# Convolution layers: where ScalarE empties the chain banks, where VectorE takes moments, and where two z products stand

## The reference, cut to what matters

```python
def conformer_conv_mixer(h, w_in, conv_w, conv_b, ln_g, ln_b, w_out):
    proj = h @ w_in
    val, glu_gate, z = jnp.split(proj, 3, axis=-1)
    u = val * jax.nn.sigmoid(glu_gate)
    u = causal_depthwise_conv(u, conv_w) + conv_b      # 31 taps per channel
    u = jax.nn.silu(layer_norm(u, ln_g, ln_b))
    return (u * jax.nn.silu(z)) @ w_out
```

## Time and profile before

| | us |
|---|---|
| median of 3 runs (2718.98 to 2719.5) | 2719.24 |
| the profiled execution | 2718.03 |
| its span, first to last instruction | 2716.3 |

### The profile page before, as it was taken

One profiled execution on the slowest core, in us unless ns is written; L12 is line 12 of the kernel. 1 busy time (PEld: TensorE's weight loads), 2 busy tenths in 40 slices (PEclk: granted clock), 3 DMA queues, 4 the chain that ended last, 5 costly groups with the idle time before them and its releaser, 6 DMA issues.

```text
span 2716.3 us, 31913 instructions
## 1 busy us (share of the span) xinstructions
PE 2599.7 (96%) x12164; PEld 2093.6 (77%) x12164; DVE 1530.4 (56%) x2443; ACT 1223.3 (45%) x1927; POOL 1496.3 (55%) x914
## 2 busy tenths in 40 slices
PE   8799999999999999999999979989999999999998
PEld 7677777777778777888888767768877778788887
DVE  4888876125856833444441788877489763432202
ACT  4686644335554633222232577654334554332322
POOL 2698846444444455444454288866634537544652
PEclk9999999999999999999999989999999999999999
DMA  5676513543344222333333567532421233232231
GB/s 149 157 159 144 127 67 86 94 101 65 76 81 66 79 71 85 100 102 93 95 103 97 124 143 168 121 96 93 129 97 63 83 106 121 79 109 93 93 104 52
DMA packets 295128, 276.51 MB, mean 102 GB/s; under 512 B 17653, under 2 KB 258511, under 8 KB 294976
## 3 DMA queue, kind: packets, MB, share of 16 engines
q1 hardware_dynamic: 280880, 223.94, 30.2%
q0 software_dynamic: 14096, 50.53, 9.0%
HBM read 228.75 MB, written 5.84 MB: 86 GB/s over the span
## 4 chain that ended last, share of the span: by engine, by line
PE 77%; DVE 16%; ACT 4%; issue 2%; POOL 1%; DMA 0%; DVEq 0%; POOLq 0%; ACTq 0%
PE ps L64 74%; DVE ps L81 7%; DVE AR L81 4%; PE ps L67 2%; DVE AR L73 2%; ACT AR L70 2%; DVE HL L81 1%; ACT L70 1%; ACT HT L70 1%; DVE X L73 1%; DVE ST L97 0%; POOL AR L73 0%; DMA AR<-in_x 0%; DVE AR L77 0%; ACT SQ L70 0%
## 5 line engine op out<-in xcount | busy, mean ns | idle before, releaser
L73 POOL TENSOR_TENSOR WL<-WR,WH 128x1024 fp32r<-128x1024 f32 x329 | 829.4, 2541 | 822.5 <-ACT WH L70 822.5
L64 PE MATMUL ps<-HH,WH 128*128 128x512 f32 x3080 | 1236.4, 401 | 20.4 <-ACT AR L70 9.4
L64 PE MATMUL ps<-HL,WH 128*128 128x512 f32 x3080 | 1209.6, 393 | 0.0
L64 PE MATMUL ps<-HH,WL 128*128 128x512 f32 x3080 | 1100.3, 390 | 0.0
L64 PEld LDWEIGHTS ps<-HH,WH 128*128 128x128 f32 x3080 | 585.3, 190 | 166.6 <-issue 21.1
L64 PEld LDWEIGHTS ps<-HL,WH 128*128 128x128 f32 x3080 | 585.4, 190 | 125.2 <-issue 7.7
L64 PEld LDWEIGHTS ps<-HH,WL 128*128 128x128 f32 x3080 | 580.1, 188 | 122.5
L70 ACT ACTIVATE WH<-WR 128x1024 fp32r<-128x1024 f32 (+1 forms) x405 | 408.6, 1046 | 464.5 <-PE ps L64 429.9
L81 DVE SCALAR_TENSOR_TENSOR ps<-AR,CW,ps 128x512 f32<-128x512 f32 x666 | 462.0, 752 | 8.8 <-ACT ps L70 1.5
L73 POOL TENSOR_TENSOR AR<-AR 128x512 f32<-128x512 f32 x194 | 274.7, 1559 | 83.3 <-ACT AR L70 76.3
L70 ACT ACTIVATE AR<-ps 128x512 f32<-128x512 f32 (+3 forms) x265 | 132.0, 522 | 299.0 <-PE ps L64 199.2
(11 more groups left out here) (169 smaller groups left out, 2278.3 us busy)
## 6 DMA issues: line engine op xcount, KB each, us to landing
WR<-in_a_w_in SPq DMA_DIRECT2D x96, 512.0 KB, 5.2
WL<-WR POOLq DMA_DIRECT2D x76, 512.0 KB, 5.1
WR<-in_c_w_in SPq DMA_DIRECT2D x64, 512.0 KB, 5.3
WR<-in_a_w_out SPq DMA_DIRECT2D x16, 1024.0 KB, 4.8
WR<-in_b_w_in SPq DMA_DIRECT2D x16, 1024.0 KB, 8.4
WR<-in_b_w_in SPq DMA_DIRECT2D x32, 512.0 KB, 12.7
WR<-in_w_mlp_in SPq DMA_DIRECT2D x16, 1024.0 KB, 5.5
WR<-in_w_mlp_out SPq DMA_DIRECT2D x16, 1024.0 KB, 4.9
```

What stands on the lines that cost most here:

```text
L64: return Op(None if self.e is None else self.e.matmul(o, l, r, start=first, stop=last, skip_group_check=True))
L73: return Op(None if self.e is None else self.e.tensor_tensor(o, a, b, op))
```

## The change

- `conv_scalar` is gone. In slots 0 to 15 ScalarE now does the starts and the first half of the products, then the sigmoid, then the begins and the second half. The emptying of banks stands at the end of the slot in all slots. For chains that end in slot 15 or later it is done two slots after their last tap.
- A bank counts as free, for the next chain and for GpSimd's last addition, when it has been emptied in an earlier slot (`emptied`), no longer when its taps have ended.
- The moments of a turn stand in the turn's own slot on VectorE, behind the first five taps (or behind all, where there are five or fewer). From slot 16 on no turn stands right behind another's slot.
- Tile 12 has 24 of its taps on GpSimd, before 18. So GpSimd makes 144 additions in a layer, before 138, and VectorE's chains have 6 taps less. GpSimd's room is 8 additions in each slot below 16 (before 7 and 8 by turns), then 3 and 4 (before 3).
- Z product 13 stands in slot 29, ahead of the last turns, and z product 14 behind the last turn and ahead of the spreads.

```diff
@@ -806,7 +806,7 @@
 
 
 
-        POOL_TAPS = {2: PAD, 4: PAD, 7: PAD, 10: PAD, 12: 18}
+        POOL_TAPS = {2: PAD, 4: PAD, 7: PAD, 10: PAD, 12: 24}
         CHAIN = [i for i in range(KE) if POOL_TAPS.get(i, 0) < PAD]
         PE_BEGINS = CHAIN[3:]
         LAST_TAP = {i: PAD - 2 if i in PE_BEGINS else PAD - 1 for i in CHAIN}
@@ -819,24 +819,25 @@
 
             taps = {i: list(range(POOL_TAPS.get(i, 0), LAST_TAP[i] + 1)) for i in CHAIN}
             adds = {i: list(range(PAD)) if POOL_TAPS[i] == PAD else list(range(1, POOL_TAPS[i])) + [PAD] for i in POOLED}
-            plan, begun, open_, ended, done, turned, pooled = [], 0, [], {}, {}, [], []
+            plan, begun, open_, ended, emptied, done, turned, pooled = [], 0, [], {}, {}, {}, [], []
             for slot in range(2 * KE + 1):
                 rest = slot == 2 * KE
-                at = {"begin": [], "tap": [], "evac": [], "start": [], "add": [], "turn": [], "moments": []}
-                at["moments"] = plan[-1]["turn"] if plan else []
-                ripe = sorted((i for i in done if done[i] + (3 if POOL_TAPS.get(i) == PAD else 1) < slot and i not in turned),
+                at = {"begin": [], "tap": [], "evac": [], "start": [], "add": [], "turn": []}
+                lately = slot >= KE and plan[-1]["turn"]
+                ripe = [] if lately else sorted((i for i in done if done[i] + (3 if POOL_TAPS.get(i) == PAD else 1) < slot and i not in turned),
                               key=lambda i: done[i])
                 at["turn"] = ripe[:1]
                 turned += at["turn"]
                 for i in CHAIN:
-                    if ended.get(i) == slot - 1:
+                    if i in ended and slot == ended[i] + (1 if ended[i] < KE - 1 else 2):
                         at["evac"].append(i)
+                        emptied[i] = slot
                         if i not in POOL_TAPS:
                             done[i] = slot
 
                 def begin():
                     i = CHAIN[begun]
-                    free = begun < 4 or ended.get(CHAIN[begun - 4], slot) < slot
+                    free = begun < 4 or emptied.get(CHAIN[begun - 4], slot) < slot
                     return i if free and i + (i >= 2) <= slot else None
 
                 while begun < len(CHAIN) and begin() is not None:
@@ -855,9 +856,9 @@
                     if i < slot and i not in pooled and len([m for m in pooled if adds[m]]) < 2:
                         pooled.append(i)
                         at["start"].append(i)
-                room = PAD * KE if rest else (7 + slot % 2) if slot < KE else (3)
+                room = PAD * KE if rest else (8) if slot < KE else (3 + slot % 2)
                 for n in range(room):
-                    two = [i for i in pooled if adds[i] and (adds[i][0] < PAD or ended.get(i, slot) < slot)]
+                    two = [i for i in pooled if adds[i] and (adds[i][0] < PAD or emptied.get(i, slot) < slot)]
                     if two:
                         i = two[n % len(two)]
                         at["add"].append((i, adds[i].pop(0)))
@@ -865,7 +866,7 @@
                             done[i] = slot
                 plan.append(at)
             assert begun == len(CHAIN) and not any(taps.values()) and not any(adds.values())
-            late = [i for i in CHAIN if ended[i] == 2 * KE]
+            late = [i for i in CHAIN if i not in emptied]
             return plan, late, [i for i in range(KE) if i not in turned]
 
         PLAN, LATE_EVAC, LATE_TURN = conv_plan()
@@ -954,7 +955,7 @@
                     product(pe, c0 + slot, 1, banks[(2 * slot + 1) % 3][:, :], gen).then_inc(a_val, j, slot)
                 elif slot < 2 * KE - Z_LATE:
                     z_tensor(pe, j, slot - KE)
-                elif slot == 2 * KE - 1:
+                elif slot == 2 * KE - Z_LATE:
                     z_tensor(pe, j, KE - 3)
                 for i in PLAN[slot]["begin"]:
                     if i in PE_BEGINS:
@@ -971,9 +972,9 @@
             wait_chain_bank(pe, j, CHAIN[-1])
             for i in CHAIN[-4:]:
                 pe.wait_ge(a_ev, j, i)
+            z_tensor(pe, j, KE - 2)
             spread(pe, ("ln", j), 1, banks[4][:, :])
             spread(pe, ("lnm", j), 0, banks[5][:, :])
-            z_tensor(pe, j, KE - 2)
             z_tensor(pe, j, KE - 1)
             project_tensor(pe, 3 * j, c0 + KE + KE // 2)
 
@@ -993,9 +994,11 @@
                     dve.wait_ge(a_val, j, slot)
                     dve.tt(U[slot][:, PAD:], banks[(2 * slot + 1) % 3][:, :], SIG[slot % 2], ALU.mult).then_inc(
                         a_u, j, slot)
-                for i in PLAN[slot]["moments"]:
-                    moments(dve, j, i)
-                for i, k in PLAN[slot]["tap"]:
+                some, turned = PLAN[slot]["tap"], PLAN[slot]["turn"] if slot < 2 * KE else []
+                for n, (i, k) in enumerate(some):
+                    if n == 5:
+                        for m in turned:
+                            moments(dve, j, m)
                     b = chain_bank(i)[:, :]
                     if k > POOL_TAPS.get(i, 0):
                         dve.wait_ge(a_tap, j, i, k - 1)
@@ -1006,6 +1009,9 @@
                             dve.wait_ge(a_init_a, j, i)
                         dve.wait_ge(a_u, j, i)
                     dve.stt(b, U[i][:, k:k + T], conv_w(j, k, i), b, ALU.mult, ALU.add).then_inc(a_tap, j, i, k)
+                if len(some) <= 5:
+                    for m in turned:
+                        moments(dve, j, m)
             for i in PLAN[2 * KE]["turn"] + LATE_TURN:
                 moments(dve, j, i)
             dve.wait_ge(a_mom, j, TURNS[-1], NB - 1)
@@ -1059,10 +1065,7 @@
             o = REST if i in POOL_TAPS else U[i][:, PAD:]
             act.act(o, chain_bank(i)[:, :], ACT.Identity, bias=a_vec("conv_b", j, i)).then_inc(a_ev, j, i)
 
-        def conv_scalar(act, j, at, some):
-            starts_scalar(act, j, at)
-            for i in at["evac"]:
-                evacuate_scalar(act, j, i)
+        def begins_scalar(act, j, at):
             for i in at["begin"]:
                 n = CHAIN.index(i)
                 if i not in PE_BEGINS:
@@ -1071,7 +1074,6 @@
                     act.act(chain_bank(i)[:, :], U[i][:, PAD:], ACT.Copy, scale=conv_w(j, PAD, i)).then_inc(a_init_a, j, i)
                 if n + 1 < len(CHAIN) and CHAIN[n + 1] in PE_BEGINS:
                     diagonals_scalar(act, j, CHAIN[n + 1])
-            products_scalar(act, j, some)
 
         def starts_scalar(act, j, at):
             for i in at["start"]:
@@ -1114,15 +1116,14 @@
                 n = PLAN[slot]["add"]
                 if slot < KE:
                     split_hi(act, c0 + slot + 1, (0, 1) if slot == 0 else (1,))
-                    if slot >= 2:
-                        conv_scalar(act, j, PLAN[slot], n[:len(n) // 2])
+                    starts_scalar(act, j, PLAN[slot])
+                    products_scalar(act, j, n[:len(n) // 2])
                     act.wait_ge(a_gate, j, slot)
                     if slot >= 2:
                         act.wait_ge(a_u, j, slot - 2)
                     act.act(SIG[slot % 2], banks[2 * slot % 3][:, :], ACT.Sigmoid).then_inc(a_sig, j, slot)
                     split_hi(act, c0 + slot + 2, (0,))
-                    if slot < 2:
-                        conv_scalar(act, j, PLAN[slot], [])
+                    begins_scalar(act, j, PLAN[slot])
                     products_scalar(act, j, n[len(n) // 2:])
                 elif slot < 2 * KE - Z_LATE:
                     m = (slot - KE) // 2
@@ -1131,9 +1132,12 @@
                     elif m + 2 < KE // 2:
                         split_hi(act, c0 + KE + m + 2, (0,))
                     silu_z(slot - KE)
-                    conv_scalar(act, j, PLAN[slot], n)
-                else:
-                    conv_scalar(act, j, PLAN[slot], n)
+                if slot >= KE:
+                    starts_scalar(act, j, PLAN[slot])
+                    begins_scalar(act, j, PLAN[slot])
+                    products_scalar(act, j, n)
+                for i in PLAN[slot]["evac"]:
+                    evacuate_scalar(act, j, i)
             for i in LATE_EVAC:
                 evacuate_scalar(act, j, i)
             rsqrt_scalar(act, ("ln", j), NB)
```

## The result

| | before | after |
|---|---|---|
| median of 4 runs each, us | 2719.15 (2718.98 to 2719.5) | 2649.77 (2649.64 to 2651.24) |
| ratio, with its 95% interval | | 0.9746 (0.9729 to 0.9763) |
| the profiled execution, us | 2718.03 | 2649.69 |
| its span, us | 2716.3 | 2648.0 |

The changed kernel is 2.5% faster: 69.4 us by the medians and 68.3 by the profiled executions. The forecast of 2655 was 5 us too high, and the time lies in its own range of 2647 to 2667.

The account below looks back on a forecast made before the run. TensorE, busy 96%, bounds the kernel; only its idle time and the slow clock behind it, 39 us a layer, can be won. Gain 31.5 a layer, twice 63, takes 2718.0 to 2655; own range 2647 to 2667, low end 2640, high end 2686.

Parts of the forecast that it names:

- ScalarE's emptying: Banks emptied at the slot's end on ScalarE: the sigmoid comes in time, TensorE's waits of 4.70 and 1.87 us go whole.
- The 4.70 and 1.87: TensorE's idle us before: a value product waiting for a sigmoid at 104.03, and a begin waiting for an emptied bank.
- VectorE's moments: Moments taken in the turn's own slot on VectorE: turn waits of 9.74, 0.98, 4.01 and 3.06 us go.
- The 9.74, 0.98, 4.01 and 3.06: TensorE's idle us before, at turns waiting for the moments of the turn before; all claimed to go.
- The tail: Layer's end on TensorE: 1.1 us gap stays before turn 12, 5.33 before spreads goes, 5.8 opens before the projection.
- GpSimd's end: GpSimd, with 6 additions more, keeps up with nothing over: last addition at 305 us, the turn needing it at 312.
- The sum: Per layer: lost before 39.2 us, left 8.6, gain 30.6; walking the slots 32.7; taken 31.5, twice 63.
- (a): Rival, chance 0.17: loading and splitting weight chunks binds GpSimd's slots, 15 us a layer less some 3 of lead; 2679.
- (b): Rival, chance 0.08: no gap ahead of the projection, so 5.8 + 1.6 us twice are won too; 2640.
- (c): Rival, chance 0.04: GpSimd becomes the bound at 1.56 us an addition, turn 12 waits 38 us; slower, 2731.
- (d): Rival, chance 0.06: stalls only move, ScalarE stalling at the slot's end until VectorE's last tap; half the gain, 2687.
- The rule of the Trainium skill: VectorE and GpSimd share an SBUF port pair as exclusive lock; a tap with one tile in PSUM takes nothing.

## Why the prediction was right, point by point

- **ScalarE's emptying.** Right. The 4.70 and 1.87 went whole, the 41.2 us of waiting for taps became 0.5, and undoing it alone brings a gap of 4.12 back in the same place. It is worth 13.1 us a layer, twice what that gap cost before with its slow product (6.5), as it brings a second late sigmoid with it.
- **VectorE's moments.** Right. My walk had u of slots 3 to 9 at 85.0, 97.5, 109.9, 123.1, 136.4, 147.0 and 158.3 us; they came at 84.8, 97.1, 109.7, 122.7, 135.7, 146.2 and 157.8. The last tap ends at 304.84 us. The 9.74, 0.98, 4.01 and 3.06 are gone; undoing this part alone costs 8.2 us a layer.
- **The tail.** Right. Slot 15 ends at 228.4 (said 229), z product 12 at 305.45 (305.7), 13 at 311.36 (311), turn 12 begins at 312.87 behind the 1.08 I had let stand. From the second spread's copy on ScalarE to tile 0's low part it is 321.64 to 332.66, 11.0 us (11.1), and the new gap is 5.71 (5.8). These rows of ScalarE and GpSimd in the changed kernel are the way that the earlier trace rows shows of before:

```profile
321.64 0.60 ACT L70 ACTIVATE AR<-ps 128x512 f32<-128x512 f32 x1 [0.26 <-PE ps L64]
...
325.88 5.28 POOL L73 TENSOR_TENSOR WL<-WR,WH 128x1024 fp32r<-128x1024 f32 x2 [13.88 <-ACT WH L70]
331.12 1.54 POOL L73 TENSOR_TENSOR HL<-AR,HH 128x512 fp32r<-128x512 f32 x1
```

- **GpSimd's end.** Off by 4.7 us without effect: its last addition ends at 309.66, not 305. From 284 us on one tile alone is left and each addition needs the one before it. Such additions start 1.37 us apart (303.51 and 304.88) where two tiles by turns give 1.25, and two z slots take 12.7 us (274.38 to 287.12) where they took the forecast 11.7 (262.67 to 274.38). That is some 2.5 us of the 4.7. Another 1.5 were lost in the two slots from 237.63, with 0.69 us of waiting for ScalarE's product. The last rows:

```profile
299.77 2.40 POOL L73 TENSOR_TENSOR WL<-WR,WH 128x1024 fp32r<-128x1024 f32 x1
...
303.51 2.67 POOL L73 TENSOR_TENSOR AR<-AR 128x512 f32<-128x512 f32 x2
...
308.38 1.28 POOL L73 TENSOR_TENSOR AR<-AR,DG 128x512 f32<-128x512 f32 x1
309.63 2.37 POOL L73 TENSOR_TENSOR WL<-WR,WH 128x1024 fp32r<-128x1024 f32 x1
```

  I had called the slack 7 us; it is 3.2, and the kernels with 28 taps and with z product 13 moved both ran into it.
- **The sum.** This is the term that was mis-sized. I had 30.6 a layer from the list of gaps and 32.7 from walking the slots, and took 31.5. The walk was right: 32.2 and 32.6 were measured, 64.8 for both layers where the sum had 63. I had put the list's shortfall down to short slow pieces that I did not list. The trace of before has none: each of its five pieces at the lower level in the layer (from 103.8, 127.7, 260.8, 335.9 and 349.6 us) stands at a listed gap. The term that was too small is the slow clock behind the gaps, 8.4 us. By the starts of the same numbered matmuls the 9.74 cost 11.75 us in all and the 4.70 cost 6.47, so 2.0 and 1.8 beyond their brackets, and the 3.06 some 1.6, where I had 1.6, 1.6 and 1.0. Gaps for which I had put nothing beyond the bracket cost some 0.2 us more too, as the 0.98 with its 1.21. The other 3.5 us came from outside the two layers, where I had looked for nothing. 1.8 + 3.5 is the miss of 5.3 us on the profiled execution. The 3.5 is chance as far as the runs show, and so the forecast was nearer in what it reasoned about (1.8 of 64.8) than its total tells.
- **The rivals.** (a) ScalarE did wait longer for weight chunks, 26.9 us in eleven waits, 5.8 at most, but TensorE's list has no `WL`; part of the time that ScalarE used to spend on taps went there. (b) fell: the gap ahead of the projection is there. (c) fell at 24 taps and showed at 28. (d) fell: ScalarE does not stall at the slot's end, as VectorE's last tap of the chain is done by then.
- **The rule of the Trainium skill.** The subtraction at 299.77 ran beside VectorE's taps and took 2.40 us; the one at 309.63 ran while VectorE mostly waited and took 2.37; the two in the tail, beside VectorE's operations on two SBUF tiles, took 5.28, 2.64 each. The Trainium skill, SBUF — State Buffer, section "SBUF: two separate sides", agrees; the denser taps did not slow GpSimd. What I had not looked at is who pays in the tail. It is VectorE. Two of its additions take 1.29 us by themselves (322.27), and six beside the subtractions 8.92:

```profile
322.27 1.29 DVE L73 TENSOR_TENSOR AR<-AR 128x512 f32<-128x512 f32 x2 [0.17 <-ACT AR L70]
324.89 8.92 DVE L73 TENSOR_TENSOR AR<-AR 128x512 f32<-128x512 f32 x6 [1.32 <-ACT AR L70]
```

  Three of the six have lengths of 2.86, 2.82 and 1.58 us, and each ends within 0.6 us behind the GpSimd operation beside it. It cost TensorE nothing here, since tile 0's way leads over GpSimd; the 0.5 us by which the two subtractions are longer lie on that way, inside the 11.0.

## What to carry to other kernels

An engine takes its instructions in order, so an instruction that waits for a slow producer belongs behind everything that somebody else waits for; look one engine further than the one that idles to find it. Before work is moved into a gap, ask which wait it covers where it stands: z product 14 closed 5.3 us and opened 5.7, and only a product that covered nothing (13) could be moved for gain. Where a list of gaps and a walk by absolute times differ, trust the walk: it holds what stands behind each gap at its full price.

## What the runs showed of the hardware

- Totals moved by 2 to 5 us with no gap to account for it: short pieces at the 1.2 GHz level fall at other places in stretches whose instructions did not change. One kernel's runs spread by up to 6.4 us (2689.79 to 2696.19) for the same reason or another; which, the runs don't settle. Below some 4 us only the layer's own timeline tells two of these kernels apart.
- A pause of TensorE costs more than its length. At full clock the projection's first product takes 5.45 us (366.62 to 372.07 in the kernel before). Behind 5.7 us of pause it took 7.12 (332.80 to 339.93) in the changed kernel and 7.2 to 8.3 in the experiments, so 1.7 to 2.8 us more. A shorter pause need not be cheaper in this: behind 2.98 us it took 8.36 in one layer and 7.16 in the other.
- Beside a GpSimd subtraction on SBUF tiles one VectorE addition of two SBUF tiles took up to 2.86 us, against 0.69 alone; the subtraction itself went from 2.40 to 2.64.
- GpSimd's 128x512 additions start 1.25 us apart on two accumulators by turns and 1.37 on one, whatever mean length the page shows, 1559 ns before and 1846 after.
